# Past keys loaded two rows to a partition, state values placed by the load, and a pair's last pages in two halves

## The chip, the cores and the metric

The kernel runs on one core of a Trainium2 chip. Each time is the device time in microseconds (us) of one execution, and lower is better. Its engines are TensorE (PE in the rows, PEld for its weight loads), VectorE (DVE), ScalarE (ACT), GpSimd (POOL) and SyncE (SP). SP computes nothing: it issues nearly all the transfers. Sixteen DMA engines carry them.

## What the kernel computes

One decoder layer, for a prompt of 512 positions and for eight sample sequences of 8 new positions each, with 4096 positions of past. Everything is float32.

```
qkv = RMSNorm(x) @ w_in                       # q, k, v of two head groups, rotary on q and k
A, 4 heads:  out = (softmax(q1 k1^T) - lambda * softmax(q2 k2^T)) v     # 2 x 64-d keys, 128-d values
   sample:   the keys and values of the past lie in pages of 128 positions,
             page_table (8 x 32) says which page of the pool
B, 8 heads:  a query at t reads the keys t, t-d, t-2d, ... down to t-window,
             (window, d) = (128,1), (512,4), (2048,16); the three parts joined by their denominators
   sample:   keys and values of the last 2048 positions: state_k_win, state_v_win (8, 2048, 8, 64)
x += concat(A, B) @ w_out;  x += SwiGLU(RMSNorm(x));  final RMSNorm
```

A page is 128 rows of 512 floats (2 KB), for keys and for values alike. The past of one sequence is 32 such pages, and the state of one sequence is 16 pages' worth of rows.

## The kernel before

**Items and slots.** The work on the samples is cut into eight items of two sequences (a pair): items 0 to 3 are group A over the past, items 4 to 7 group B over the state. Each item is cut into groups ("quads") of four pages for each of its two sequences. An item of the past has 8 such quads. An item of the state has only the rows that some window reads, which is 3: two whole quads and a last one of two pages for each sequence (`pages_of` is 2 there, and 4 elsewhere). That makes `KSLOTS` = 44 quads. A slot t has eight steps i. In slot t the keys of quad t are scored, and the values of quad t - `LAG` (`LAG` = 8) are weighed, so slots 0 to 51 do attention for the samples, slots 0 to 31 score the past, slots 8 to 39 weigh the past, and slots 40 to 51 weigh the state. Beside this, "pieces" of the prompt's work (projection, attention, output projection) are dealt out over the same steps (`SHARE`). After the last slot comes the feed-forward part, which needs everything before it.

**Keys.** `load_keys(t, i)` on SP loads page i (0 to 3 for the first sequence, 4 to 7 for the second) of quad t into `k_ring[:, i, :]`, which has one place for each of the eight pages, once the DVE has turned the page of quad t - 1 in that place (`kt_done`). `load_page` issues the transfer: a page of the past goes row by row to 128 partitions, a pair of the state's pages in one transfer of two neighbouring rows (4 KB) to each of 128 partitions (`state_pair`), and each of a last quad's pages as `[4, 32]` rows of 2 KB. `turn_page` (L2153) transposes each page in blocks of 32x32 into `kt_sb`. `score_keys` (L1232) multiplies 32 times for each half of a quad into the bank `S`, four products side by side, and `keep_scores` (L2190) brings the scores with their mask from `S` to `s_sb`, four instructions for a quad.

**Values.** `load_values(t, h)` on SP loads the four pages of sequence h for slot t. Where they lie goes by `ring_of`: `v_ring` up to slot 43, then by turns `k_ring`, `v_ring` and `t_ring`, which lies where `kt_sb` was. `place_values` (L666) puts row (b, j) of page k on partition 4j + k at place b. For a last quad each of the two pages goes as 32 rows of 8 KB to every second one of 64 partitions. From slot 47 on ACT issues the second half's transfers (in `evac_probs`). `turn_probs` (L1245) transposes the weights four times, `evac_probs` (L1693) copies them to `pt_sb`, and `weigh_values` (L1270) multiplies 32 times for each half, after it has waited for all pages of the half; `pv_half[h]` then counts it.

**Order.** Every engine follows its own list of steps, written out by the loops over t and i. On SP a step of slot t holds, in this order: keys of quad t + 1 (i below 4) or of quad t + 2 (i from 4), the transfers of the pieces, the second half's values of slot t at i = 0, and the first half's values of slot t + 1 at i = 6. SP does one thing after the other, and a wait in front of a transfer holds all behind it. From slot 43 on values are loaded two to three slots ahead. In slot 45 the first 1 MB of the gate weights (`g_raw`) is loaded, in slot 48 the first 1 MB of the up weights. The transfers that SP issues pass through the DMA engines in the order of issue.

## Time and profile before

| | us |
|---|---|
| median of 3 runs | 1122.25 |
| lowest, highest | 1115.1, 1124.65 |
| the profiled execution: its time | 1113.92 |
| the profiled execution: its span | 1112.1 |

| engine | busy us | share of the span |
|---|---|---|
| PE | 969.6 | 87% |
| DVE | 668.9 | 60% |
| ACT | 505.7 | 45% |
| POOL | 133.9 | 12% |

In 40 slices of 27.8 us each, the share of DMA busy time (in tenths) reads `8699999999999999888979798386768686974632`, and what was moved (GB/s) lies between 310 and 365 from the third slice to the sixteenth. The samples' attention lasts to 697 us, which is slice 25, and the feed-forward part follows. 311 MB are moved in all, by 174,933 packets. A DMA share of 1.0 means that all 16 engines had a packet under way all the time. It is worked out from the packets' own durations and can come out a little above 1. SP has no busy time in the profile, since issuing is not counted as such. Its transfers stand in the lists of instructions as SPq.

### The profile page before, as it was taken

How to read it: one execution, taken by the hardware profiler on the slowest of the kernel's cores; microseconds unless marked ns; L12 is line 12 of the kernel's file. 1: busy time of each engine (PE TensorE's matmuls, PEld its weight loads, DVE VectorE, ACT ScalarE, POOL GpSimd, SP SyncE). 2: the span in 40 equal slices, each digit the busy share in tenths (PEclk: the TensorE clock that was granted, in tenths of full speed). 3: DMA queues.
4: the chain of work that ended last, by engine and by line, in shares of the span. 5: the costliest groups of instructions: out<-in, count | busy, mean ns of one | idle time of the engine just before them, and what ended most of it. 6: DMA issues, size and time to landing. Idle time of an engine off the chain costs nothing.

```text
span 1112.1 us, 29337 instructions
## 1 busy us (share of the span) xinstructions
PE 969.6 (87%) x11050; PEld 858.7 (77%) x11050; DVE 668.9 (60%) x1627; ACT 505.7 (45%) x1116; POOL 133.9 (12%) x69
## 2 busy tenths in 40 slices
PE   3989898998887779887889667899999999999995
PEld 3978787777764557676667554699999999999994
DVE  5389645675458887754346445788888888700003
ACT  5654543374125656645234262455555555611123
POOL 1322111111000010002111000000000000133330
PEclk8999999999988999888899787899999999999997
DMA  8699999999999999888979798386768686974632
GB/s 249 248 314 346 320 328 344 358 340 334 317 340 338 337 365 329 301 273 293 327 245 298 221 255 223 123 302 264 301 263 301 263 301 252 325 248 159 228 128 85
DMA packets 174933, 310.98 MB, mean 280 GB/s; under 512 B 13601, under 2 KB 87714, under 8 KB 173282
## 3 DMA queue, kind: packets, MB, share of 16 engines
q1 hardware_dynamic: 172898, 305.24, 80.3%
q10 hardware_dynamic: 1920, 4.20, 1.4%
q8 instruction: 74, 1.21, 0.4%
q14 instruction: 41, 0.34, 0.1%
HBM read 302.30 MB, written 73.92 MB: 338 GB/s over the span
## 4 chain that ended last, share of the span: by engine, by line
PE 32%; issue 30%; DMA 11%; SPq 11%; DVE 7%; ACT 7%; ACTq 0%; POOL 0%; DVEq 0%; POOLq 0%
PE ps L1383 11%; DMA v_ring<-in_cache_v_diff 6%; SPq L666 5%; PE ps L1038 5%; PE ps L1270 4%; PE ps L1232 4%; SPq L768 4%; DVE kt_sb L2153 2%; ACT q_st L1678 2%; PE ps L1189 2%; DMA k_ring<-in_state_v_win 2%; DMA k_ring<-in_cache_k_diff 2%; PE ps L1115 1%; DMA v_ring<-in_state_v_win 1%; ACT s_sb L1723 1%
## 5 line engine op out<-in xcount | busy, mean ns | idle before, releaser
L2153 DVE STREAM_TRANSPOSE kt_sb<-k_ring 128x512 f32<-128x512 f32 x336 | 220.5, 691 | 86.5 <-DMA k_ring<-in_cache_k_diff 37.4
L1270 PE MATMUL ps<-v_ring,pt_sb 128*32 128x128 f32 (+1 forms) x2496 | 98.8, 306 | 62.1 <-DMA v_ring<-in_cache_v_diff 49.3
L1270 PEld LDWEIGHTS ps<-v_ring,pt_sb 128*32 128x32 f32 (+1 forms) x2496 | 75.7, 121 | 78.1 <-issue 67.8
L1038 PE MATMUL ps<-h_hi,w_hi 128*128 128x288 f32 x384 | 124.4, 324 | 1.9 <-DVE h_lo L2006 1.9
L1038 PE MATMUL ps<-h_lo,w_hi 128*128 128x288 f32 x384 | 115.0, 299 | 0.0
L1038 PE MATMUL ps<-h_hi,w_lo 128*128 128x288 f32 x384 | 114.7, 299 | 0.0
L1232 PE MATMUL ps<-kt_sb,q_st 128*32 128x128 f32 (+1 forms) x2816 | 97.0, 281 | 10.2 <-DVE q_st L2163 4.6
L989 POOL TENSOR_TENSOR c_lo<-c_raw,c_hi 128x1408 fp32r<-128x1408 f32 x14 | 46.6, 3332 | 440.2 <-ACT c_hi L1781 440.2
L1232 PEld LDWEIGHTS ps<-kt_sb,q_st 128*32 128x32 f32 x2816 | 72.9, 114 | 28.2 <-issue 19.9
L1038 PEld LDWEIGHTS ps<-h_hi,w_hi 128*128 128x128 f32 x384 | 74.0, 193 | 16.1 <-issue 13.8
L949 POOL TENSOR_TENSOR w_lo<-w_raw,w_hi 128x1024 fp32r<-128x1024 f32 x24 | 57.3, 2390 | 229.5 <-ACT w_hi L1492 229.5
L1693 ACT ACTIVATE pt_sb<-ps 128x512 f32<-128x512 f32 (+1 forms) x44 | 26.2, 594 | 129.2 <-PE ps L1245 129.2
L1320 PE MATMUL ps<-t_h,s_h 128*128 128x288 f32 x264 | 77.9, 295 | 1.2 <-ACT u L1774 1.2
L1320 PE MATMUL ps<-t_l,s_h 128*128 128x288 f32 x264 | 77.9, 295 | 0.0
L1320 PE MATMUL ps<-t_h,s_l 128*128 128x288 f32 x264 | 77.7, 294 | 0.0
L2444 DVE TENSOR_TENSOR x<-x,ps 128x512 f32 (+1 forms) x8 | 5.5, 689 | 119.5 <-PE ps L1396 119.5
L2292 DVE TENSOR_TENSOR s_l<-s_t,s_h 128x512 fp32r<-128x512 f32 x88 | 58.8, 689 | 28.4 <-ACT s_h L1745 18.1
L1383 PE MATMUL ps<-a_hi,c_hi 128*128 128x288 f32 x352 | 75.4, 296 | 0.2 <-POOL c_lo L989 0.2
L1383 PE MATMUL ps<-a_lo,c_hi 128*128 128x288 f32 x352 | 75.3, 295 | 0.0
L1383 PE MATMUL ps<-a_hi,c_lo 128*128 128x288 f32 x352 | 74.9, 294 | 0.0
L1038 PEld LDWEIGHTS ps<-h_lo,w_hi 128*128 128x128 f32 x384 | 74.3, 194 | 0.0
L1038 PEld LDWEIGHTS ps<-h_hi,w_lo 128*128 128x128 f32 x384 | 73.9, 192 | 0.0
(236 smaller groups left out, 2289.4 us busy)
## 6 DMA issues: line engine op xcount, KB each, us to landing
k_ring<-in_cache_k_diff SPq DMA_DIRECT2D x256, 256.0 KB, 5.5
v_ring<-in_cache_v_diff SPq DMA_DIRECT2D x256, 256.0 KB, 5.5
out_k_win_sample<-in_state_k_win SPq DMA_DIRECT2D x32, 1020.0 KB, 8.3
out_v_win_sample<-in_state_v_win SPq DMA_DIRECT2D x32, 1020.0 KB, 8.5
k_ring<-in_state_k_win SPq DMA_DIRECT2D x32, 512.0 KB, 7.7
w_raw<-in_w_in SPq DMA_DIRECT2D x24, 512.0 KB, 6.3
g_raw<-in_w_gate SPq DMA_DIRECT2D x11, 1024.0 KB, 5.2
g_raw<-in_w_up SPq DMA_DIRECT2D x11, 1024.0 KB, 5.2
```

What stands on the lines that cost most here:

```text
L666: queue.dma_start(dst, src).then_inc((k_landed, v_landed, t_landed)[ring][i], 16)
L768: sp.dma_start(k_ring[:, at_first:i + 1, :].squeeze(1) if at_first == i else k_ring[:, at_first:i + 1, :], src)\
L949: nc.gpsimd.tensor_tensor(w_lo[:, n % 3, :], w_raw[:, n % 3, :], w_hi[:, n % 2, :].bitcast(F32), ALU.subtract).then_inc(w_lo_done, 1)
L989: nc.gpsimd.tensor_tensor(c_lo[j][:, 0:width], c_raw[:, j, 0:width], c_hi[j][:, 0:width].bitcast(F32), ALU.subtract).then_inc(w_lo_done, 1)
L1038: last = nc.tensor.matmul(M[c][:, 0:HALF], wt, act[:, k, c * HALF:(c + 1) * HALF], start=k == 0 and at_first, stop=k == KT - 1 and act is ...
L1232: last = nc.tensor.matmul(S[32 * f:32 * f + 32, c0:c0 + 32 * n], q_st[:, h, f, r, :], kt_sb[:, 4 * h:4 * h + n, c:c + 32], start=r % 2 == ...
L1270: last = nc.tensor.matmul(O[32 * f:32 * f + 32, P * h:P * h + P], pt_sb[0:rows, 4 * f + b, :], values[:, f * P:(f + 1) * P], start=g == 0 ...
L1320: last = nc.tensor.matmul(ps[:, bank, 0:HALF], wt[:, k, :], act[:, k, :], start=j in (0, 1, 3) and k == 0 and at_first, stop=k == 3 and wt ...
L1383: last = nc.tensor.matmul(main_ps[:, 2 * bank + c, 0:HALF], wt[j][:, w], a_lo[:, pair, block, :] if low else a_hi[pair][:, block, :], star ...
L1693: nc.scalar.activation(pt_sb[r].rearrange("p m (k t) -> p k m t", k=4), X[r].rearrange("p (k m t) -> p k m t", k=4, t=DT), ACT.Copy).then_ ...
L2153: V.transpose(kt_sb[:, i, :], k_ring[:, i, :]).then_inc(kt_done, 1)
L2292: V.tensor_tensor(dst[:, :, :], src, high[:, :, :].bitcast(F32), ALU.subtract).then_inc(form_low, 1)
```

## The change

Four things change together.

1. **Keys of the past**: page i of a pair (i, i + 1) no longer fills the 128 partitions of its own place. Its rows 2u and 2u + 1, 4 KB that lie side by side in memory, go to the two places of the pair on partition 2u + (i mod 2). A transfer is then 64 rows of 4 KB to every second partition, and a place holds half of each of two pages. `turn_page` waits for both pages of the pair, `load_keys` waits until both places of the pair have been turned, `kt_sb` takes the places in the order 0, 2, 1, 3, and `score_keys` writes its 128 columns of `S` in pairs of two, eight columns apart, so that the scores come out in the order of the positions. `keep_scores` then reads and writes them in a row.
2. **Values of the state, whole quads**: `place_state` replaces `place_values`. One transfer is now one place b: 32 stretches of 8 KB in memory, one 2 KB row to each of 128 partitions. `weigh_values` waits for each place just before the four products that read it, not for the whole half first.
3. **A pair's last pages**: both sequences of the pair share one half of `v_ring` (half 0 or 1 by the item's number), the first on partitions 0 to 63, the second on 64 to 127. Two transfers of 512 KB (source `h j (b c)`, with h = 2, j = 32 and 8 KB in a row) replace four of 256 KB. Their weights are transposed by two instructions instead of four, and copied by two (64 rows by 256) instead of one. PE waits for its own first half before the second.
4. **Where they are issued**: the last pages of slot 48 are issued at slot 44, step 0 instead of slot 45, step 6, and those of slot 51 at slot 45, step 6 instead of slot 48, step 6. ACT no longer issues any for these two slots. For slots 42 and 45 the step stays. The loads after a last quad's slot in the same ring wait for its second half.

The diff, cut to its core:

```diff
@@ -131,6 +131,13 @@
 return 512 * g + (0 if it < 4 else WCOLS * ((it - 4) % 3))
+def part0(q, k):
+it, g = item_of(q)
+return col0(it, g) + (P * k if pages_of(q) == 4 else 64 * (2 * (k % 2) + k // 2))
...
@@ -658,12 +665,24 @@
     h, k = divmod(i, 4)
-    n = pages_of(q)
-    if n == 4:
-        src = src.rearrange("(b j) c -> j b c", b=4)
-    rows, ring = slice(k, 32 * n, n), ring_of(q + LAG)
+    rows, ring = slice(k, P, 4), ring_of(q + LAG)
     dst = (k_ring[rows, 4 * h:4 * h + 4, :], v_ring[rows, h, :, :], t_ring[rows, h, :, :])[ring]
-    queue.dma_start(dst, src).then_inc((k_landed, v_landed, t_landed)[ring][i], 16)
+    queue.dma_start(dst, src.rearrange("(b j) c -> j b c", b=4))\
+        .then_inc((k_landed, v_landed, t_landed)[ring][i], 16)
+def place_state(queue, q, h, x):
+    it, g = item_of(q)
+    b, ring = 2 * (it - 4) + h, ring_of(q + LAG)
+    if pages_of(q) == 4:
+        dst = (k_ring[:, 4 * h + x, :], v_ring[:, h, x, :], t_ring[:, h, x, :])[ring]
+        queue.dma_start(dst, sv[b, 32 * x:32 * x + 32, 4 * g:4 * g + 4, :])\
+            .then_inc((k_landed, v_landed, t_landed)[ring][4 * h + x], 16)
+    else:
+        src = sv[b:b + 2, 96:P, 8 + 4 * x:12 + 4 * x, :].rearrange("h j b c -> h j (b c)")
+        queue.dma_start(v_ring[x:P:2, it % 2, :, :].rearrange("p b c -> p (b c)"), src).then_inc(v_landed[4 * (it % 2) + x], 16)
...
@@ -757,41 +776,56 @@
             src = (ck if keys else cv)[ds(ids[keys, h][4 * (g % 2) + k], 1)].squeeze(0)
-        else:
-            src = state_rows(sk if keys else sv, q, i)
+        elif keys:
+            src = state_rows(sk, q, i)
         if keys:
             if n == 2:
                 src = src.rearrange("p j c -> j p c")
             elif it >= 4:
                 src = state_pair(sk, q, i)
-            at_first = i - (it >= 4 and n == 4)
-            sp.dma_start(k_ring[:, at_first:i + 1, :].squeeze(1) if at_first == i else k_ring[:, at_first:i + 1, :], src)\
-                .then_inc(k_landed[i], 16)
+            if it < 4:
+                dst, src = k_ring[i % 2:P:2, i - i % 2:i - i % 2 + 2, :], src.rearrange("(u r) c -> u r c", r=2)
+            else:
+                dst = k_ring[:, i - 1:i + 1, :] if n == 4 else k_ring[:, i, :]
+            sp.dma_start(dst, src).then_inc(k_landed[i], 16)
+        elif it < 4:
+            place_values(sp, q, i, src)
         else:
-            place_values(sp, q, i, src)
+            place_state(sp, q, h, k)
     def load_keys(t, i):
         if has_k(t) and i % 4 < pages_of(t) and key_load(t, i) == i:
             if t:
                 last, h = t - 1, i // 4
-                sp.wait_ge(kt_done, PAGE_NO[last, i] + 1 if i % 4 < pages_of(last) else half_end(last, h))
+                sp.wait_ge(kt_done, PAGE_NO[last, i | 1] + 1 if i % 4 < pages_of(last) else half_end(last, h))
             load_page(True, t, i)
     def load_values(t, h):
+        q = t - LAG
+        if pages_of(q) == 2:
+            if h == 0:
+                half = item_of(q)[0] % 2
+                q0 = {FIRST[4] + 2: q - 1, FIRST[5] + 2: q - 2, FIRST[6] + 2: q - 5, FIRST[7] + 2: q - 6}[q]
+                sp.wait_ge(pv_half[half], q0 + 1)
+                for x in range(2):
+                    place_state(sp, q, h, x)
+            return
         if t == KSLOTS:
             sp.wait_ge(kt_done, half_end(KSLOTS - 1, h))
-        elif t == KSLOTS + 1:
-            sp.wait_ge(pv_half[h], t - LAG - 1)
         elif t == KSLOTS + 2:
             sp.wait_ge(scored if h else half_scored, KSLOTS)
         elif t > KSLOTS + 2:
-            sp.wait_ge(pv_half[h], t - LAG - 2)
+            sp.wait_ge(pv_half[h], q - 2)
         elif t > LAG:
-            sp.wait_ge(pv_half[h], t - LAG)
-        for k in range(pages_of(t - LAG)):
-            load_page(False, t - LAG, 4 * h + k)
+            sp.wait_ge(pv_half[1 if pages_of(q - 1) == 2 else h], q)
+        for k in range(4):
+            load_page(False, q, 4 * h + k)
...
@@ -889,9 +923,12 @@
                 load_values(KSLOTS + 2, 1)
-                load_values(KSLOTS + 1, 1)
+                load_values(KSLOTS + 4, 0)
+            if (t, i) == (KSLOTS + 1, 6):
+                load_values(KSLOTS + 7, 0)
             if i == 6 and t >= KSLOTS and has_v(t + 3):
-                load_values(t + 3, 0)
+                if pages_of(t + 3 - LAG) == 4:
+                    load_values(t + 3, 0)
...
@@ -1229,7 +1266,12 @@
                 c = 32 * (4 * f + r)
-                last = nc.tensor.matmul(S[32 * f:32 * f + 32, c0:c0 + 32 * n], q_st[:, h, f, r, :],
+                scores = S[32 * f:32 * f + 32, c0:c0 + 32 * n]
+                if it < 4:
+                    scores = scores.rearrange("p (u x c) -> p x u c", x=4, c=2)
+                last = nc.tensor.matmul(scores, q_st[:, h, f, r, :],
...
@@ -1240,9 +1282,9 @@
             pe.wait_ge(x_free, X_NO["p", t])
-        for k in range(4):
-            c = col0(it, g) + 32 * n * k
-            last = nc.tensor.transpose(X[0:32 * n, k * P:(k + 1) * P], s_sb[:, c:c + 32 * n], ident[:, :])
+        for k in range(n):
+            c = col0(it, g) + P * k
+            last = nc.tensor.transpose(X[:, k * P:(k + 1) * P], s_sb[:, c:c + P], ident[:, :])
...
@@ -1256,18 +1298,27 @@
         it, g = item_of(q)
-        rows = 32 * pages_of(q)
+        n = pages_of(q)
+        rows, at = (slice(0, P), h) if n == 4 else (slice(64 * h, 64 * h + 64), it % 2)
         pe.wait_ge(x_free, X_NO["p", t] + 1)
         if g == 0 and h == 0 and it:
             pe.wait_ge(o_scaled, it)
         ring = ring_of(t)
         landed = (k_landed, v_landed, t_landed)[ring]
-        for k in range(pages_of(q)):
-            pe.wait_ge(landed[4 * h + k], V_LANDS[q, 4 * h + k])
+        if n == 2 and h == 1:
+            pe.wait_ge(pv_half[0], q + 1)
+        by_place = it >= 4 and n == 4
+        if not by_place:
+            for k in range(n):
+                pe.wait_ge(landed[4 * at + k], V_LANDS[q, 4 * at + k])
         for b in range(4):
-            values = (k_ring[0:rows, 4 * h + b, :], v_ring[0:rows, h, b, :], t_ring[0:rows, h, b, :])[ring]
+            if by_place:
+                pe.wait_ge(landed[4 * h + b], V_LANDS[q, 4 * h + b])
+            values = (k_ring[rows, 4 * at + b, :], v_ring[rows, at, b, :], t_ring[rows, at, b, :])[ring]
             for f in range(4):
-                last = nc.tensor.matmul(O[32 * f:32 * f + 32, P * h:P * h + P], pt_sb[0:rows, 4 * f + b, :],
+                last = nc.tensor.matmul(O[32 * f:32 * f + 32, P * h:P * h + P], pt_sb[rows, 4 * f + b, :],
...
@@ -1278,6 +1329,10 @@
         pe.wait_ge(y_free, Y_NO["g", 2 * s + 1] + 1)
+        if it >= 4:
+            pe.wait_ge(pv_half[1], FIRST[it] + QUADS[it])
...
@@ -1689,12 +1744,19 @@
             act.wait_ge(pv_half[1], q)
-        r = slice(0, 32 * pages_of(q))
-        nc.scalar.activation(pt_sb[r].rearrange("p m (k t) -> p k m t", k=4),
-                             X[r].rearrange("p (k m t) -> p k m t", k=4, t=DT), ACT.Copy).then_inc(x_free, 1)
+        into = pt_sb[:].rearrange("p m (k t) -> p k m t", k=4)
+        if pages_of(q) == 4:
+            last = nc.scalar.activation(into, X.rearrange("p (k m t) -> p k m t", k=4, t=DT), ACT.Copy)
+        else:
+            for h in range(2):
+                r = slice(64 * h, 64 * h + 64)
+                last = nc.scalar.activation(into[r, 2 * h:2 * h + 2],
+                                            X[r, 0:2 * P].rearrange("p (k m t) -> p k m t", k=2, t=DT), ACT.Copy)
+        last.then_inc(x_free, 1)
         if t > KSLOTS and has_v(t + 2):
-            for k in range(pages_of(q + 2)):
-                place_values(act, q + 2, 4 + k, state_rows(sv, q + 2, 4 + k))
+            if pages_of(q + 2) == 4:
+                for b in range(4):
+                    place_state(act, q + 2, 1, b)
...
@@ -2146,11 +2208,12 @@
             return
-        at_load = key_load(t, i)
-        dve.wait_ge(k_landed[at_load], K_LANDS[t, at_load])
+        for page in (i - i % 2, i | 1) if t < FIRST[4] else (key_load(t, i),):
+            dve.wait_ge(k_landed[page], K_LANDS[t, page])
         if t:
             dve.wait_ge(scored if i >= 4 else half_scored, t)
-        V.transpose(kt_sb[:, i, :], k_ring[:, i, :]).then_inc(kt_done, 1)
+        to = i - i % 4 + (0, 2, 1, 3)[i % 4] if t < FIRST[4] else i
+        V.transpose(kt_sb[:, to, :], k_ring[:, i, :]).then_inc(kt_done, 1)
...
@@ -2186,10 +2249,11 @@
         for k in range(4):
-            c = col0(it, g) + 32 * n * k
-            last = V.tensor_tensor_reduce(out=s_sb[:, c:c + 32 * n].rearrange("p (j x) -> p j x", x=n),
-                                          in0=S[:, 32 * n * k:32 * n * (k + 1)].rearrange("p (x j) -> p j x", x=n),
-                                          in1=mask.rearrange("p (j x) -> p j x", x=n), scale=1.0, scalar=-3e38,
+            c = part0(t, k)
+            x = n if it >= 4 else 1
+            last = V.tensor_tensor_reduce(out=s_sb[:, c:c + 32 * n].rearrange("p (j x) -> p j x", x=x),
+                                          in0=S[:, 32 * n * k:32 * n * (k + 1)].rearrange("p (x j) -> p j x", x=x),
+                                          in1=mask.rearrange("p (j x) -> p j x", x=x), scale=1.0, scalar=-3e38,
```

## Rows read from the trace of the kernel before

**Rows 1.** Windows (us): busy us of each engine (instructions), granted clock, DMA share, GB/s.
```profile
95.00:130.00 35.00, 32.56 (x462) 29.32 (x463) 30.24 (x83) 16.39 (x40) 7.18 (x3) 1.00 1.03 349
...
360.00:440.00 80.00, 65.26 (x1048) 48.68 (x1049) 66.54 (x227) 48.80 (x149) 7.01 (x12) 0.96 0.99 347
```

**Rows 2.** All waits of the SP queue, 130 to 440 us: total us, times, longest.
```profile
SPq L756 <- DVE kt_sb L2153: 4.1, 10, 0.6
SPq L666 <- PE ps L1270: 2.1, 1, 2.1
SPq L756 <- PE ps L1270: 0.8, 1, 0.8
```

**Rows 3.** Chain of waits: first-half scores of slots 7 and 31 (start, us, what).
```profile
118.99 1.01 PE ps L1232 x32
...
445.55 1.01 PE ps L1232 x32
```

**Rows 4.** SP's transfers in order of time: start, length of the group in us.
```profile
370.70 2.97 SPq L666 DMA_DIRECT2D v_ring<-in_cache_v_diff  x4
373.85 4.04 SPq L768 DMA_DIRECT2D k_ring<-in_cache_k_diff  x6
378.64 3.00 SPq L666 DMA_DIRECT2D v_ring<-in_cache_v_diff  x4
382.15 1.37 SPq L768 DMA_DIRECT2D k_ring<-in_cache_k_diff  x2
```

**Rows 5.** By tile: issue time in ns, min/median/max.
```profile
L768 SPq DMA_DIRECT2D k_ring<-in_cache_k_diff x256: 332/333/2361, 21.5 to 439.7; - x128
...
L666 SPq DMA_DIRECT2D v_ring<-in_cache_v_diff x256: 602/602/2186, 53.8 to 572.1; - x128
...
L714 SPq DMA_DIRECT2D x<-in_x_sample x2: 471/523/575, 3.5 to 696.0; - x2
```

**Rows 6.** Window in which only rows of 4 KB are loaded; columns as in rows 1.
```profile
5.00:10.00 5.00, 0.00 (x0) 0.00 (x0) 0.31 (x2) 2.29 (x5) 0.00 (x0) 1.00 0.95 358
```

**Rows 7.** Waits of the DVE's page transposes, and form of the score products.
```profile
DVE kt_sb L2153 <- DMA k_ring<-in_cache_k_diff: 37.4, 28, 2.7
...
L1232 PE MATMUL ps<-kt_sb,q_st 128*32 128x128 f32 x2560 | 91.4, 286 | 10.2 <-DVE q_st L2163 4.6 <-issue 2.9 <-DVE kt_sb L2153 2.7
```

**Rows 8.** SP's transfers round the first last quad's values.
```profile
601.56 3.88 SPq L768 DMA_DIRECT2D k_ring<-in_state_k_win  x4
607.29 1.16 SPq L666 DMA_DIRECT2D v_ring<-in_state_v_win  x2
611.47 0.58 SPq L768 DMA_DIRECT2D k_ring<-in_state_k_win  x1
612.10 1.13 SPq L666 DMA_DIRECT2D v_ring<-in_state_v_win  x2
613.27 0.58 SPq L768 DMA_DIRECT2D k_ring<-in_state_k_win  x1
```

**Rows 9.** Windows: last quad's keys under way, and the highest rate; columns as in rows 1.
```profile
616.00:624.00 8.00, 3.48 (x57) 2.82 (x61) 2.08 (x7) 1.08 (x3) 0.00 (x0) 0.71 0.29 80
...
548.00:550.00 2.00, 1.97 (x37) 1.61 (x37) 0.74 (x2) 0.30 (x1) 2.00 (x1) 1.00 1.05 406
```

**Rows 10.** Chain of waits near the end of attention: start, us, what.
```profile
612.62 12.28 DMA v_ring<-in_state_v_win
...
668.57 18.71 DMA k_ring<-in_state_v_win
687.42 1.86 PE ps L1270 x32
...
696.99 270.26 issue
```

**Rows 11.** Windows near the end of attention; columns as in rows 1.
```profile
650.00:660.00 10.00, 7.82 (x150) 6.19 (x152) 5.66 (x13) 6.14 (x15) 0.00 (x0) 1.00 1.04 299
...
680.00:690.00 10.00, 6.74 (x139) 5.00 (x137) 3.65 (x7) 1.55 (x2) 0.00 (x0) 0.88 1.01 208
```

More of the change, by code:

```diff
@@ L300, in landings @@
         for i in range(8):
-            if i % 4 < pages_of(q):
+            if pages_of(q) == 4 or i - 4 * (item_of(q)[0] % 2) in (0, 1):
                 here = seen[ring_of(q + LAG)]
@@ L1717, in exps @@
                     if it >= 4 and half:
-                        at0 = col0(it, 2) + 64 * k
+                        at0 = part0(FIRST[it] + 2, k)
                         part = s_sb[:, at0:at0 + 64]
```

## The prediction

> **What bounds the kernel now.** I read the windows over the stage of the past's keys first. The DMA share stands at 0.99 to 1.03 and 347 to 349 GB/s [rows 1], so all sixteen DMA engines have a packet under way nearly all the time, while PE and DVE each have gaps. Next the waits of SP: 7.0 us in 310 us [rows 2]. SP hardly ever waits for a buffer. The chain of waits gives the length of a slot: from slot 7 to slot 31 it is (445.55 - 118.99) / 24 = 13.6 us [rows 3]. Last SP's own list: between 370.70 and 384.27 us it issues eight value and eight key transfers, just one slot's worth, and that takes 13.57 us [rows 4]. So SP's round of issuing is as long as the slot. Two things are at their limit at once: the DMA engines, and the queue that feeds them. The small slack of SP shows in the same rows. A key's issue takes 333 ns in the median, and some 0.19 us of register work stands beside it, but the six keys took 4.04 us where 6 x 0.52 = 3.1 us would do: one issue was held about 1 us because the engines took no more.
>
> After slot 41 it is other things. The chain has single landings of 12.28 and 18.71 us [rows 10], at windows where the DMA share is 1.0 and only 208 to 299 GB/s move [rows 11], or where the share is 0.29 with 80 GB/s [rows 9]. The second kind of window is the one to understand: a share of 0.29 is 4.6 of 16 engines. What was issued before it are last quads' keys [rows 8], whose source is written as 4 x 32 x 512, the 4 in front. Four engines carry such a transfer, and the values issued behind it (at 612.62) land only at 624.9, since the same four engines must do their part of them too.
>
> **Keys of the past, bytes.** 256 transfers of 256 KB, 67 MB, go by 4 KB instead of 2 KB. The window with rows of 4 KB moves 358 GB/s at a share of 0.95 [rows 6], which is 377 GB/s if full, against 347 at 0.99 now [rows 1]. 67 MB take 193 us at the one rate and 178 at the other, so the engines are relieved of at most 15 us, 0.5 us per slot. I take nothing of it, since SP's round is as long as the slot: the engines gain slack that nobody fills.
>
> **Keys of the past, issuing.** The transfer is now 64 rows to every second partition. No row of this trace has that form. The full 128 partitions in a row cost SP 333 ns; 32 rows to every fourth partition cost 602 ns; 64 rows to partitions in a row cost 471 and 575 ns [rows 5]. Both neighbours in the number of rows and in the step are dear, and I take 0.60 us, the row with a partition step. That is 8 x 0.27 = 2.1 us more of SP per slot, less the 1.0 us of slack: 1.1 us for each of the 24 slots with keys and values of the past, 25 us. Low end: at 471 ns it is 1.1 us per slot, which the slack takes, and with it the engines' relief could show, -12 us. High end: no slack is usable, 24 x 2.1 = 50 us. The first eight slots have no values to issue, and SP has room there.
>
> **Keys of the past, waits.** A key load waits for the second turn of its pair. Behind it on SP stand at step 0 the four value loads of the second half. SP waits 7 us in all today, and it lags behind the DVE, so I put this at nothing. If that cover is gone, it is up to one page turn (0.7 us) per half quad, within the high end. On the DVE the first turn of a pair waits for the page that is issued second, four value issues (3 us) later. The DVE already waits 37.4 us for keys [rows 7], the turns of the later pages come as before, and what hides it is that scores need all four pages. Zero; up to 0.7 us a half if not.
>
> **Scores.** 32 products per half quad take 1.01 us [rows 3]. They now write `S` in pairs of columns, eight apart. No product in this trace writes PSUM with a stride, so the cost lies between nothing and twice the time, 1 us for 64 halves. PE is 93% busy in slots 0 to 7 and 82% later [rows 1]. I take nothing, the pairs being what the form keeps together. The Trainium skill's page "PSUM — Partial Sum Buffer" (Specifications) says that any non-contiguous pattern slows matmuls significantly, which would be the other end; no run here shows it yet. The DVE's reading in a row saves next to nothing on an engine that is not the last.
>
> **State values, whole quads.** 48 transfers of the same 256 KB with 2 KB to each of 128 partitions. I take the same issue time and bytes. PE can begin when the first place has landed, so behind the last landing stand 4 of 16 products instead of all: up to 0.8 us at each of some four landings in the chain, -3 us.
>
> **A pair's last pages.** This is the large term. Before: 16 transfers, 4.2 MB on all engines at 208 to 299 GB/s [rows 11], 14 to 20 us. Now: 8 transfers of 512 KB whose source is 2 x 32 x 2048, the 2 in front. What a 4 in front does is in rows 8 and 9; by the same form a 2 in front gives two engines. One engine moves at best 406 / (16 x 1.05) = 24 GB/s [rows 9] and, with company, 80 / 4.6 = 17 GB/s. So 1.05 MB of one item take 1.05 / (2 x 24) = 22 us on two engines, and up to 31 us. The Trainium skill's page "DMA: Bandwidth & Descriptors" (Why a DMA increments its semaphore by 16 and not by 1) states it as a rule: the largest number up to 16 that divides both slowest dimensions, which makes 2 of 2 and 64; the trace agrees as far as the 4.6 engines go.
>
> These two engines carry their part of everything else, in the order of issue. From the first such load (at about 607 us [rows 8]) to the last landing that attention needs they have: 4 x 22 = 88 us of last pages; four key loads of the last quad, 1.05 MB at 80 GB/s, 13 us, half of it done before; 48 value loads, 12.6 MB at 347 GB/s, 36 us; 2.1 MB of weights, 6 us. That is 137 us, to about 744. Now the last landing is at 687.3 us [rows 10]. With some of it overlapped by ACT's own queue I take +50 us. Low end +30, if early issue hides one item's load; high end +75 at 17 GB/s. The move of slots 48 and 51 to an earlier step does not help, because the loads issued behind them (values of slots 46, 47, 49, 50, the weights) pass the same two engines first come, first served. PE and ACT follow each landing in order. The feed-forward part starts when attention ends and moves with it.
>
> The rest (two transposes and one wait on itself fewer or more on PE, two small copies instead of one on ACT in four slots, four issues of 0.6 us less on ACT) is about 2 us in all, either way.
>
> **Sum** against the profiled execution: 1113.9 + 25 + 50 - 3 = 1186 us. Its 1113.9 is 8 us below the median of the runs shown, 1122.25, so the change against the median could read a few us less.
>
> **Rivals.** (a) Only the two engines bite; a strided key load costs SP no more than its slack. For it: the slack is there. Against: both near forms are dear. 1113.9 + 50 - 3, less 8 for the relief: 1153 us. (b) The two-sequence load is spread over all sixteen engines after all, and only the issuing grows: last pages in long rows to all 128 partitions gain 5 us (14 to 20 us down to 12), so 1113.9 + 25 - 5 - 3 = 1131 us. Against it stand the 4.6 engines. (c) Faster: the change does what its form promises. It decides by two conditions: issue stays near 333 ns and the last pages spread. Then the engines' relief shows, 12 us, and with the 5 and the 3 it is 1094 us. (d) The strided writing of scores doubles them. PE at 93% in slots 0 to 7 has no room for 2 us in 8, later SP's longer round covers it: 10 us more than forecast, 1196 us.
>
> **Numbers.** Forecast 56%, (a) 18%, (b) 10%, (c) 8%, (d) 6%, something else 2%. The forecast's own range is 1160 to 1228. For 8 in 10 I take in (a) and (d) and leave out (b) and (c): 1138 to 1228. About 1%, 11 us round 1122, is what a measurement of this kernel can tell from no change. Slower by more: forecast, (a), (d), nearly half of (b), half of the rest: 85%. Within: 7%. Faster: 8%.
>
> **What would show it.** Key issues of the past near 600 ns and slots 8 to 31 at 14.7 us or so instead of 13.6, with a DMA share under 0.97. After 607 us, long windows with a share of 0.13 to 0.3 and values that take 20 us or more to land; the end of attention at about 770 us. Score halves still at 1.01 us. Wrong if the share stays near 1 in both stages, if the landings of last pages take under 10 us, or if slots stay at 13.6 us.

## The result, and the profile after

The changed kernel takes 1213.91 us (median of 6 runs, 1210.73 to 1218.03) against 1116.94 us of the kernel before on the same chip (6 runs, 1111.86 to 1124.65). The ratio is 1.0864, with a 95% interval of 1.0817 to 1.0911: slower by 8.6%. The profiled execution took 1213.99 us, and its span is 1212.2 us. That is 100 us more than the profiled 1113.9 of before. I had forecast 72 us more. Both halves of the change cost time where the prediction put it, and both cost more than I gave them.

Windows of the changed kernel: the stage of the past, and three stretches near the end of attention. The columns are those of [rows 1].

```profile
130.00:440.00 310.00, 245.81 (x3606) 199.81 (x3605) 186.38 (x559) 129.47 (x333) 33.74 (x20) 0.93 0.93 313
652.00:670.00 18.00, 0.14 (x2) 0.00 (x0) 2.60 (x8) 1.35 (x3) 0.00 (x0) 0.57 0.17 64
700.00:718.00 18.00, 1.51 (x14) 1.20 (x12) 1.19 (x6) 3.26 (x8) 0.00 (x0) 0.66 0.33 110
740.00:800.00 60.00, 30.56 (x390) 17.20 (x392) 16.48 (x38) 9.00 (x16) 0.00 (x0) 0.61 0.34 103
```

In the first row the DMA share is 0.93 and 313 GB/s move, where the same window of before has 0.99 and 338 GB/s. The DMA engines have gaps now. In the second row the share is 0.17, that is 2.7 of 16 engines, while PE is busy for 0.14 us of 18.

SP's round in the changed kernel, to be laid beside [rows 4]:

```profile
375.80 3.03 SPq L670 DMA_DIRECT2D v_ring<-in_cache_v_diff  x4
379.01 1.88 SPq L792 DMA_DIRECT2D k_ring<-in_cache_k_diff  x2
381.63 3.02 SPq L670 DMA_DIRECT2D v_ring<-in_cache_v_diff  x4
384.83 5.04 SPq L792 DMA_DIRECT2D k_ring<-in_cache_k_diff  x6
```

The eight value issues take 6.05 us, as they did (5.97). The eight key issues take 6.92 us where they took 5.41. Issue times by tile (ns, min/median/max), answering [rows 5]:

```profile
L792 SPq DMA_DIRECT2D k_ring<-in_cache_k_diff x256: 474/484/1501, 22.4 to 472.3; - x128
L670 SPq DMA_DIRECT2D v_ring<-in_cache_v_diff x256: 602/613/1865, 54.3 to 608.9; - x128
L681 SPq DMA_DIRECT2D v_ring<-in_state_v_win x24: 536/603/1582, 616.2 to 680.7; - x24
L685 SPq DMA_DIRECT2D v_ring<-in_state_v_win x8: 522/2084/15949, 643.9 to 745.1; - x8
```

A key issue went from 333 to 484 ns in the median, not to 600. The last row is the surprise. Eight issues of the last pages have a median of 2.1 us, and one of them took 15.9 us. The chain of waits of the changed kernel at the end of attention (start, us, what), answering [rows 10]:

```profile
644.47 26.52 DMA v_ring<-in_state_v_win
...
690.24 28.23 DMA v_ring<-in_state_v_win
718.61 1.93 PE ps L1321 x32
...
732.55 12.51 SPq L685
...
748.76 31.97 DMA t_ring<-in_state_v_win
...
796.90 270.34 issue
```

Three landings of 26.5 to 32.0 us stand where two of 12.28 and 18.71 us stood. The first two are of last pages; the third is of a whole quad's places, issued right behind the fourth pair's last pages. Attention ends at 796.9 us, not at 697.0. What follows is as long as before (270.34 us, 270.26 before), so the whole difference arises ahead of that point.

I divide it by stages. The table has, in us and for the profiled execution of each kernel (e1 to e9b are the experiments below), when the score products of the first half of slots 7, 31 and 42 begin, when attention ends, and the stretch between the last two.

| kernel | slot 7 | slot 31 | slot 42 | attention ends | slot 42 to the end |
|---|---|---|---|---|---|
| before | 119.0 | 445.5 | 614.1 | 697.0 | 82.9 |
| after | 123.7 | 479.1 | 650.7 | 796.9 | 146.2 |
| e1 key part alone | 124.2 | 483.5 | 659.3 | 738.1 | 78.8 |
| e2 without the key part | 121.8 | 446.0 | 615.3 | 758.7 | 143.4 |
| e3 after, last values spread | 123.9 | 479.7 | 656.2 | 733.6 | 77.4 |
| e4 before, last keys spread | 120.2 | 452.1 | 607.3 | 687.6 | 80.3 |
| e5 before, more reads by SP | 120.7 | 470.8 | 641.0 | 716.5 | 75.5 |
| e6 after, ACT issues values | 125.6 | 465.1 | 655.4 | 800.1 | 144.7 |
| e7 before, ACT issues values | 118.8 | 450.4 | 637.2 | 718.2 | 81.0 |
| e8 after, both spread | 120.9 | 475.7 | 631.1 | 704.0 | 72.9 |
| e9b e2, both spread | 122.9 | 448.3 | 603.8 | 674.8 | 71.0 |

Before to after: 5 us by slot 7, 29 us in slots 8 to 31 (14.8 us a slot, 13.6 before), 3 us to slot 42, and 63 us from there to the end. The column of slot 7 scatters: it runs from 118.8 to 122.9 in the kernels without the key part and from 120.9 to 125.6 in those with it, so little can be read from those 5 us.

### The profile page after: what moved, and what is told of

It reads as the page before. It is cut to its first block, busy times and chain, and to the rows that moved or that the text cites. A ratio compares the mean times of both kernels' runs of the same rounds, so it can differ in the third digit from the quotient of the medians.

```text
span 1212.2 us, 29309 instructions
## 1 busy us (share of the span) xinstructions
PE 982.1 (81%) x11042; PEld 862.6 (71%) x11042; DVE 668.2 (55%) x1627; ACT 506.9 (42%) x1120; POOL 134.4 (11%) x69
## 3 DMA queue, kind: packets, MB, share of 16 engines
q8 instruction: 74, 1.21, 0.4%
## 4 chain that ended last, share of the span: by engine, by line
issue 30%; SPq 25%; PE 18%; DMA 18%; DVE 5%; ACT 3%; POOL 0%; ACTq 0%; DVEq 0%; POOLq 0%
PE ps L1438 10%; SPq L670 10%; SPq L792 8%; DMA k_ring<-in_cache_k_diff 6%; DMA v_ring<-in_state_v_win 5%; DMA v_ring<-in_cache_v_diff 3%; PE ps L1321 3%; DMA t_ring<-in_state_v_win 3%; SPq L775 2%; DVE kt_sb L2216 2%; SPq L685 1%; DMA k_ring<-in_state_k_win 1%; SPq L681 1%; PE ps L1226 1%; SPq L860 1%
## 5 line engine op out<-in xcount | busy, mean ns | idle before, releaser
L1321 PEld LDWEIGHTS ps<-v_ring,pt_sb 128*32 128x32 f32 (+1 forms) x2496 | 73.2, 118 | 136.7 <-issue 124.0
L1274 PE MATMUL ps<-kt_sb,q_st 128*32 128x128 f32 (+1 forms) x2816 | 100.4, 287 | 8.8 <-DVE q_st L2226 4.2
L1274 PEld LDWEIGHTS ps<-kt_sb,q_st 128*32 128x32 f32 x2816 | 75.6, 117 | 28.1 <-issue 18.0
L1749 ACT ACTIVATE pt_sb<-ps 128x512 f32<-128x512 f32 x40 | 23.8, 595 | 136.7 <-PE ps L1287 136.7
L1438 PE MATMUL ps<-a_hi,c_hi 128*128 128x288 f32 x352 | 75.5, 296 | 0.2 <-POOL c_lo L1026 0.2
```

The lines of the kernel that those rows point to most:

```text
L1274: last = nc.tensor.matmul(scores, q_st[:, h, f, r, :], kt_sb[:, 4 * h:4 * h + n, c:c + 32], start=r % 2 == 0, stop=r % 2 == 1)
L1321: last = nc.tensor.matmul(O[32 * f:32 * f + 32, P * h:P * h + P], pt_sb[rows, 4 * f + b, :], values[:, f * P:(f + 1) * P], start=g == 0 an ...
L1438: last = nc.tensor.matmul(main_ps[:, 2 * bank + c, 0:HALF], wt[j][:, w], a_lo[:, pair, block, :] if low else a_hi[pair][:, block, :], star ...
```

## The experiments

**Each half alone.** Experiment e1 is the kernel before with only the key part.

Its core, beside which the waits on SP and the DVE are for both pages of a pair:

```diff
+dst, src = k_ring[i % 2:P:2, i - i % 2:i - i % 2 + 2, :], src.rearrange("(u r) c -> u r c", r=2)
+scores = scores.rearrange("p (u x c) -> p x u c", x=4, c=2)
+to = i - i % 4 + (0, 2, 1, 3)[i % 4] if t < FIRST[4] else i
...
```

> The kernel before with the key part of the change alone (past keys two rows to a partition, scores written strided, DVE and SP wait for a pair of pages); the state's values and the last pages stay as before. The theory that the change has two separate costs, SP's longer key issues while the past is read and the two-engine loads at the end, expects only the first: slots 8 to 31 at 14.8 us instead of 13.6, score halves of slot 31 about 33 us later than before, about 1117 + 35 = 1152 us. If the whole loss came from the end (rival), 1117 to 1125 us. If the key part also delays the last state pages (rival), up to 1180 us.

Measured: 1154.2 us (4 runs) against 1115.52 of before (7 runs), ratio 1.0311, interval 1.0235 to 1.0387. That is 39 us, and the slots 8 to 31 are 15.0 us long. The stretch from slot 42 to the end is no longer than before. Experiment e2 is the opposite: the changed kernel with those lines taken back.

> The changed kernel with its key part undone: past keys one row to a partition by 128-partition loads, scores written plainly; the state's values by place and the last pages in two halves stay. Theory of two separate costs: slots 8 to 31 back at 13.6 us, and the whole loss after slot 41: 1117 + 60 = 1177 us. Rival, the end is slow only because the past ends late: at most 1135 us.

Measured: 1175.94 us, ratio 1.0539 (1.0475 to 1.0603), 60 us over before. Up to slot 42 the table shows it as fast as the kernel before, and then it loses 60 us. The last two long landings of its chain and the end of attention (start, us, what):

```profile
655.60 29.11 DMA v_ring<-in_state_v_win
...
713.88 31.80 DMA t_ring<-in_state_v_win
...
758.69 270.23 issue
```

39 and 60 make 99, and the whole change costs 97. The two halves are separate costs, which follow each other in time and simply add.

**The last pages over more engines.** Experiment e3 changes in the changed kernel how the last value pages are written as transfers. With it PE waits, for each sequence, for that sequence's two transfers, and no longer for those of both.

```diff
-src = sv[b:b + 2, 96:P, 8 + 4 * x:12 + 4 * x, :].rearrange("h j b c -> h j (b c)")
-queue.dma_start(v_ring[x:P:2, it % 2, :, :].rearrange("p b c -> p (b c)"), src)
+for s in range(2):
+    src = sv[b + s, 96:P, 8 + 4 * x:12 + 4 * x, :].rearrange("j b c -> j (b c)")
+    queue.dma_start(v_ring[64 * s + x:64 * s + 64:2, it % 2, :, :].rearrange("p b c -> p (b c)"), src)
```

> The changed kernel with each load of a pair's last value pages (64 rows of 8 KB, both sequences) issued as two loads of 32 rows, one for each sequence, so that the slowest dimension of the source is 32 and not 2. The bytes, the places in SBUF and SP's order are the same; 16 issues take the place of 8. Theory that these loads are slow because two DMA engines carry them: the windows at a share near 0.13 vanish and the time falls by 40 to 60 us from 1214, to 1155 to 1175 us. Rival, that the end is slow because SP's order and waits were changed there: at least 1200 us.

Measured: 1150.08 us, ratio to before 1.0311 (1.0246 to 1.0375). Against the changed kernel's 1213.91 it is 64 us less, 5 us more than I had expected at most. The window from the first last pages to the end of attention, in the changed kernel and then in e3 (columns as in [rows 1]), and the issue times of the transfer in e3:

```profile
644.00:797.00 153.00, 70.58 (x1020) 47.89 (x1019) 39.84 (x117) 33.39 (x72) 0.00 (x0) 0.65 0.41 132
```

```profile
650.00:735.00 85.00, 57.74 (x1021) 39.77 (x1021) 41.00 (x121) 33.41 (x72) 0.00 (x0) 0.83 0.80 239
```

```profile
L686 SPq DMA_DIRECT2D v_ring<-in_state_v_win x16: 519/594/4467, 649.4 to 701.6; - x16
```

The mean share doubles from 0.41 to 0.80, 239 GB/s move where 132 did, and the held issues shrink from a median of 2084 ns to 594. The same bytes to the same places, in twice as many transfers: that takes back the whole loss of this half. The order and the waits that the change gave SP are still in e3, so they are not the cause.

The packets in the trace show the number of engines more directly. Near the end of attention only the last value pages go in packets of 8 KB, 128 for each pair. In the changed kernel the 128 of the first pair lie between 650.05 and 670.53 us, and the sum of their durations is 2.0 times that stretch: two are under way nearly all the time. The next three pairs' packets take 24.9, 26.4 and 28.4 us. In e3 the four pairs take 10.6, 6.8, 6.6 and 9.1 us, with a sum of 6.2 to 10.7 times the stretch.

**The same fault in the kernel before.** In [rows 8 and 9] the last key pages go by transfers with a 4 in front. Experiment e4 is the kernel before with each of them as four.

```diff
 if n == 2:
-    src = src.rearrange("p j c -> j p c")
+    for j in range(4):
+        sp.dma_start(k_ring[32 * j:32 * j + 32, i, :], src[:, j, :]).then_inc(k_landed[i], 16)
+    return
```

> The kernel before with each load of a last key page (slowest dimension 4, four DMA engines) issued as four loads of 32 rows of 2 KB: 64 issues for 16. If the number of engines matters already in the kernel before, where its chain has 18.71 us of one such load, it gets 5 to 15 us faster (1102 to 1112 us). If those loads are slow for what else is queued, or the added issues (48 of 0.33 to 0.6 us, 16 to 29 us of SP) weigh more, 1115 to 1130 us.

Measured: 1095.62 us (5 runs, 1091.8 to 1104.58), ratio 0.9794 (0.9736 to 0.9852), 20 us faster than the kernel before although SP issues 48 transfers more. I had expected 5 to 15. The rows of the page transposes' waits for these pages, first in the kernel before, then in e4 (us in total, times):

```profile
  DMA k_ring<-in_state_k_win: 21.0, 13
```

```profile
  DMA k_ring<-in_state_k_win: 7.8, 8
```

The table shows where it comes from: from slot 31 to slot 42 e4 takes 155 us, before 169. Its attention ends only 9 us earlier, not 20: the profiled execution is the slowest of the five, and it was 7 us late at slot 31, where the edit changes nothing yet.

**Is it SP's time?** The key part changes three things at once: the time of an issue, the form of the rows, and the waits. Experiment e5 adds time on SP to the kernel before and touches nothing else.

```diff
-if k == 0 and g % 2 == 0:
-    first = (2 * it + h) * NPAGES + 4 * g
+if k == 0:
+    first = (2 * it + h) * NPAGES + 4 * (g - g % 2)
```

> The kernel before, with SP reading the page numbers of each stream in every slot instead of every second one. No transfer, place or wait changes. Four reads of 0.525 us are added per two slots, 1.05 us of SP a slot, about what the changed key issues cost (6.9 us for eight in place of 5.4). Theory that the key part's loss is SP's time: slots 8 to 31 go from 13.6 to about 14.6 us and the time to about 1117 + 30 = 1147 us. Rival, that the loss is in the transfer (rows of 4 KB to every second partition) or in the wait for a pair: 1117 us within its spread.

Measured: 1140.1 us, ratio 1.0243 (1.0179 to 1.0308), 25 us over before. The added reads and the stage of the past (the row of the page numbers' tile; the window as in [rows 1]):

```profile
L756 SPq TENSOR_LOAD <-page_ids x128: 519/525/1582, 21.9 to 595.3; - x128
```

```profile
130.00:440.00 310.00, 250.48 (x3667) 204.22 (x3667) 185.75 (x554) 128.75 (x328) 33.08 (x20) 0.91 0.95 314
```

64 more reads of 0.525 us are 33.6 us, and 25 of them (20 to 34 by the interval) came out at the end. Slots 8 to 31 grew by 0.98 us for 1.05 us of dose. The share and the rate fell to 0.95 and 314 GB/s, the picture of the changed kernel, with not one transfer changed.

Set the key part beside it. I added up the durations of all of SP's instructions in the records, from the scores of slot 7 to those of slot 31 (us for a slot):

| kernel | SP's instructions | length of a slot | difference |
|---|---|---|---|
| before | 11.21 | 13.61 | 2.40 |
| e2 without the key part | 11.17 | 13.51 | 2.34 |
| e5 more reads | 12.24 | 14.59 | 2.35 |
| after | 12.42 | 14.81 | 2.39 |
| e1 key part alone | 12.62 | 14.97 | 2.35 |

A slot is SP's own work and 2.3 to 2.4 us in all five, whether that work is added by reads or by the key part. So SP's time is the cause in this stage, and what the waits for a pair could add beyond it is 0.1 us a slot at most. Of the 1.21 us a slot that the changed kernel has more, 0.86 us are the key issues, whose mean goes from 451 to 550 ns. The rest is on other instructions of SP: in these slots a value issue has a median of 627 ns where it had 602, and an issue of `w_raw` one of 579 where it had 427. Why these are longer no run shows. Over all 256 key issues the sum grows by 23 us in the changed kernel (113.4 to 136.8) and by 30 in e1 (143.1). The difference of the medians, 151 ns, times 256 is 38.7 us, and that it meets the 39 us of e1 is chance: the medians leave out the held issues, and there is less of those once the issue itself is longer.

**Relieving SP.** Experiments e6 (on the changed kernel) and e7 (on the kernel before) let ACT issue the second sequence's past values, four of a slot's sixteen pages. ACT reads eight page numbers in every second slot for it.

```diff
+def act_values(q):
+...
+    act.wait_ge(pv_half[1], q)
+    for k in range(4):
+        place_values(act, q, 4 + k, cv[ds(act_ids[0][4 * (g % 2) + k], 1)].squeeze(0))
```

> The changed kernel with the second sequence's past values (four of a slot's sixteen page loads) issued by ACT, which reads those page numbers itself; SP issues the rest. SP loses about 2.4 + 0.3 us a slot, ACT gains them. Theory that SP's time makes the slots longer: slots 8 to 31 fall from 14.8 to 13.6 us or less and the time by 30 us or more, to at most 1184 us. Rival, the transfer with rows of 4 KB is the slower part: slots stay at 14.8 us, 1205 to 1220 us. ACT's own work may also be held up by its issues, in which case it is slower than 1214 us.

> The kernel before with the same four loads a slot on ACT. If the slots before are set by the DMA engines (share 0.99 of their time, 349 GB/s), 1110 to 1120 us and slots of 13.6 us. If they are set by SP's time, as the experiment with the key part alone hints (its longer issues lengthened the slots in full), the slots shorten toward 12 us and the time falls to 1075 to 1100 us.

Measured: e6 1218.26 us, ratio 1.0927 (1.0847 to 1.1008), no gain; e7 1136.78 us, ratio 1.0173 (1.0107 to 1.0238), a loss of 22 us. By the whole times my expectation fell, and in e7 slots 8 to 31 are 13.8 us long where they were 13.6. In e6 they are 14.1, where they were 14.8. The windows tell more. First the changed kernel, then e6, then before, then e7, each for 130 to 300 us:

```profile
130.00:300.00 170.00, 143.90 (x2089) 124.33 (x2089) 93.43 (x251) 74.14 (x158) 26.02 (x11) 0.96 0.95 317
```

```profile
130.00:300.00 170.00, 152.01 (x2251) 131.95 (x2240) 100.34 (x271) 76.66 (x167) 28.45 (x12) 0.96 1.01 351
```

```profile
130.00:300.00 170.00, 150.72 (x2227) 130.81 (x2226) 94.27 (x245) 72.47 (x148) 28.43 (x12) 0.97 0.99 334
```

```profile
130.00:300.00 170.00, 155.91 (x2323) 135.35 (x2321) 96.27 (x259) 72.59 (x151) 28.49 (x12) 0.98 1.03 355
```

With SP relieved the rate rises from 317 to 351 and from 334 to 355 GB/s, and the share reaches 1.01 and 1.03. From slot 7 to slot 20 a slot of e6 takes 13.55 us where the changed kernel takes 14.84 and the kernel before 13.85; e7 takes 13.26. So SP set the pace there in the changed kernel, and to some part in the kernel before. It also shows that rows of 4 KB raise the rate by nothing in this stretch: 351 against 355 GB/s. From slot 20 to slot 31 the gain is gone: 14.85 us in e6 and 14.47 in e7, against 14.78 and 13.32. From slot 31 to slot 42 both take 18 to 19 us longer than the kernels that they start from. SP's own work in slots 8 to 31 is now 9.8 us a slot in e6 and 9.0 in e7, 4.4 and 4.9 us less than the slot, so over the whole stage SP no longer sets the pace. What the relief gave was lost again, and the waits point to ACT. Its longest wait in e6, and SP's in e6 and in e7, 130 to 440 us:

```profile
ACT feat L1559 <- issue: 52.9, 9, 10.8
```

```profile
SPq L792 <- DVE kt_sb L2234: 38.9, 24, 4.9
```

```profile
SPq L768 <- DVE kt_sb L2171: 49.8, 29, 4.4
```

SP now waits 38.9 and 49.8 us for page transposes; before it hardly waited at all [rows 2]. ACT's evacuation of the projections stands 52.9 us behind something that the profile calls issue, which I take to be ACT's new wait for the second half's products with four issues of 610 ns behind it. I did not test other places for it in ACT's order, so whether a better place would keep the gain stays open.

**Together.** Experiment e9 has the state's values by place, no key part, and both kinds of last pages spread; e9b is the same kernel measured again; e8 is the whole changed kernel with both spread. The edits are those of e3 and e4.

> Values by place, without the key part, with the last value pages as two loads of 32 rows a piece and the last key pages as four loads of 32 rows. If the separate effects add (the spread value loads give back 64 of 1176 us, the spread key loads 20), 1117 - 5 - 20 = about 1092 us; if values by place are worth nothing over the kernel before, equal to 1095.6 us of the kernel before with spread keys.

> The kernel of values by place, no key part, both kinds of last pages spread, once more in five rounds, to stand beside the next: 1092 to 1096 us.

> The changed kernel whole, key part included, with the last value pages as two loads of 32 rows a piece and the last key pages as four loads of 32 rows: it differs from the kernel of the experiment before (values and keys spread, 1093.8 us) by the key part alone. If the key part's cost is SP's time per past page and is untouched by what happens at the end, 1094 + 37 = 1131 us. If the relief at the end had absorbed some of it, 1095 to 1115 us.

Measured: e9 1093.79 us, ratio 0.9807 (0.9757 to 0.9856); e9b 1091.51 us, ratio 0.9789 (0.9745 to 0.9834). e8 1122.6 us in the median of nine runs (1123.78 with a tenth of 1140.08), ratio 1.0074 (1.0039 to 1.0109). So the best version is 2% faster than the kernel before and 10% faster than the changed one. Of this gain e4 alone has all: its ratio is 0.9794, and those of e9 and e9b are 0.9807 and 0.9789. Values by place, once spread, are thus worth nothing that can be measured. The key part costs 31 us in this surrounding, less than the 39 of e1 and the 37 that I expected, and the repaired change as a whole gains nothing over the kernel before. The window of e9b from slot 42 to the end of attention, and its longest landing there in the chain of e9:

```profile
600.00:675.00 75.00, 53.55 (x966) 36.32 (x958) 39.37 (x115) 33.41 (x72) 0.00 (x0) 0.84 0.84 258
```

```profile
633.14 17.46 DMA g_raw<-in_w_gate
```

258 GB/s stand where the changed kernel has 132 between 644 and 797 us. What ends last there is now a weight load.

**The other way for SP.** Experiment e10 is e9 with the keys' page numbers read sixteen at a time in every fourth slot.

```diff
-if k == 0 and g % 2 == 0:
+span = 4 if keys else 2
+if k == 0 and g % span == 0:
...
+        page_ids[0:1, first:first + 4 * span]
```

> The same with SP reading the keys' page numbers sixteen at a time in every fourth slot, instead of eight in every second. The opposite dose to the experiment that added reads: if a read of sixteen takes as long as one of eight (0.525 us), SP has 0.26 us less a slot, and at the slope measured there (25 us for 1.05 us a slot) the time falls by 6 us, to about 1088 us. If a read takes longer with its count, or DMA (share 0.98) is the limit now, no difference.

Measured: 1093.87 us, ratio 0.9804 (0.975 to 0.9857), no different from e9b. A read of sixteen takes 974 ns in the median, one of eight 525, so SP saved about 0.04 us a slot, where I had hoped for 0.26. The experiment did not give the dose that it was meant to give, and says nothing on the limit.

## Why the prediction was right or wrong

**The direction and its two places: right.** Both mechanisms of the forecast were there: each has an experiment that leaves the other half out (e1, e2), the two engines one that takes them away (e3), and SP's time one that adds nothing else (e5). Rivals (a), (b) and (c) fall with e1 and e2. The measured 1213.91 lies in the range. The forecast was 28 us low: 14 us in the key half, and 10 to 14 in the other.

**Keys of the past, issuing: 25 us forecast, 39 measured.** In the slots that the sum is about it came out nearly right, by luck: 1.1 us a slot forecast, 1.20 measured (1.36 in e1). Two errors cancel there. The price of an issue was too high: +0.27 us taken, +0.15 measured in the median, so the form of 64 rows to every second partition lies at the neighbour with 64 rows, not at the one with the partition step [rows 5]. And of the 1.0 us a slot that I took off as slack, only 0.4 could be used. Eight key issues of the kernel before are held 0.94 us in all (a mean of 451 ns in these slots over the median of 333), those of the changed kernel still 0.53 (550 over 484). So 1.2 us of price less 0.4 of slack is about the 0.86 measured, and 0.35 on SP's other instructions, which my sum did not have, makes up the rest. Taken with the measured price, my own slack would have left 0.2 us a slot, or 5 us in all: the slack is the term that failed. Outside these slots I gave nothing, and there stand some 8 us in the profiled execution of the changed kernel (5 by slot 7, within the scatter of that column, and 3 to slot 42), and 6 to 10 by the whole times (39 less 29 to 33). The first 64 of the 256 key issues are in that part. How that cost comes about the runs do not show.

**Keys of the past, bytes: nothing taken, nothing there.** I allowed the engines a relief of up to 15 us. e6 and e7 show 351 GB/s with rows of 4 KB and 355 without. The 377 GB/s that I worked out from one window at the start [rows 6] did not come again in this stage.

**Keys of the past, waits: nothing taken.** SP's waits are 8.1 us in 310 us in the changed kernel, 7.0 before. The accounting by SP's time leaves them 0.1 us a slot at most, but no run has the pair's waits alone.

**Scores: nothing taken, right.** The product's form in the stage of the past, before and after (ns, min/median/max):

```profile
L1232 PE MATMUL ps<-kt_sb,q_st x1408: 269/273/423, 136.2 to 434.2; 128*32 128x128 f32 x176
```

```profile
L1274 PE MATMUL ps<-kt_sb,q_st x1504: 269/273/423, 133.5 to 479.9; 128*32 128x128 f32 x188
```

273 ns with pairs of columns eight apart, 273 ns in a row. This disposes of rival (d). The Trainium skill's page "PSUM — Partial Sum Buffer" (Specifications) says that any non-contiguous pattern slows matmuls significantly; for this pattern the measurement says otherwise. Its page "Advanced Engine Details and Errata" (PSUM Cachelines) adds that every two consecutive elements should be contiguous for best throughput, and with that half of its rule the rows agree. Whether single columns would be slower no run here shows.

**A pair's last pages: 50 us forecast, 60 to 64 measured.** The number of engines was right: the share of 0.17 is 2.7 of 16 engines, and e3 takes the loss away by the spread alone. The Trainium skill's page "DMA: Bandwidth & Descriptors" (Why a DMA increments its semaphore by 16 and not by 1) gives the number of engines as the largest up to 16 that divides both slowest dimensions; the two packets at a time in the changed kernel agree with it, and so do the times of e3 and e4, which change these dimensions and with them the number of transfers. The 22 us for a pair were right where two engines had little else to carry: 20.5 us for the packets of the first. The sum of 137 us for these engines was right too. In e2, where the past ends as before, the first such load is issued at 608.5 us and the last long landing of the chain comes at 745.7, against a forecast of 607 and 744. In the changed kernel it is 643.9 and 780.7, again 137 us. Whether every part of that sum is right singly no run shows. What was off is what I made of it. I let 7 us of the added 57 overlap, and they did not: in e2 the last landing comes 58.4 us later than before. SP itself was held, its last-page issues took up to 15.9 us, and the values of the next slots stood unissued behind them. And I gave nothing to what PE and the others do behind the last landing: that is 9.7 us before, 13.0 in e2 and 16.2 in the changed kernel. Part of it is PE's clock. The granted clock in the windows above is 0.57 to 0.66, and half of a slot's products take 1.93 us in the chain there, 1.05 to 1.08 us in the stages where PE is busy. But the kernel before has products of 1.86 us there as well [rows 10]. How much of the added 3.3 to 6.5 us is the clock and how much is work piled up, no run shows.

**State values, whole quads: -3 us forecast.** e9 and e9b have ratios of 0.9807 and 0.9789, e4 has 0.9794: nothing that can be told from the spread.

## What to carry to other kernels

Before a transfer is rewritten for longer rows, write down its source as the list of its dimensions and look at the one in front: in this kernel two engines carried a transfer with a 2 there and about four (4.6 by the share) one with a 4, and everything that shared them waited. Splitting it into more issues with 32 in front was worth 64 us in one case and 20 in the other. Where the queue that issues is as busy as the engines that it feeds, price every issue by its form, and count a stall of the queue inside such a round as slack only in part: here 0.4 of 0.94 us. Compare sums or means of issue times, not medians alone, for the medians leave the held issues out.

## What the runs showed of the hardware

- The time of an issue depends on the form. The same 256 KB cost SP 333 ns as 128 rows to partitions in a row, 474 to 484 ns as 64 rows of 4 KB to every second partition, and 602 ns as 32 x 4 rows to every fourth. A quarter of a last key page, 32 rows of 2 KB or 64 KB to partitions in a row (e4), costs 422 ns in the median, more than the 333 ns of four times the bytes over 128 rows.
- The issuing queue is held while transfers over two engines are outstanding. The issues of the changed kernel around the third and fourth pair of last pages (SP in order of time; start, length of the group):

```profile
698.85 16.86 SPq L685 DMA_DIRECT2D v_ring<-in_state_v_win  x2
715.75 10.41 SPq L681 DMA_DIRECT2D k_ring<-in_state_v_win  x4
...
729.11 19.60 SPq L685 DMA_DIRECT2D v_ring<-in_state_v_win  x2
748.76 11.38 SPq L681 DMA_DIRECT2D t_ring<-in_state_v_win  x4
760.18 15.17 SPq L681 DMA_DIRECT2D k_ring<-in_state_v_win  x4
```

  The two issues of a pair took 16.86 and 19.60 us together, and groups of four issues of 256 KB behind them, which take 2.5 us elsewhere, 10 to 15. Transfers over all engines are held as well as those over two.
- A share near 1.0 was not the ceiling: 334 GB/s at 0.99 in the kernel before, 355 GB/s at 1.03 with a second queue issuing.
- Reading page numbers into registers goes by the number: 525 ns for eight, 974 ns for sixteen.
